# A mixture-of-experts trunk: the first expert's rows by one-hot products, and weights that no longer wait for a gather

## The reference, cut to what matters

```python
scores = softmax(xt @ router_w)                       # 512 x 16
sel = scores + router_bias
# best of 4 groups by the sum of its two best, then the two best experts in it
gates = two chosen scores, divided by their sum, 0 elsewhere
h = silu(xt @ w_gate[e]) * (xt @ w_up[e])             # 16 experts, 1024 -> 512
h = h * gates[:, e]
y = sum over e of h @ w_down[e]                       # 512 -> 1024
```

## Time and profile before

| | |
|---|---|
| median of three runs | 1234.52 us (1226.4 to 1235.66) |
| the profiled execution's own time | 1230.52 us |
| its span | 1228.8 us |
| PE busy | 1193.8 us (97%) |
| DVE, ACT, POOL busy | 893.2 us (73%), 703.7 us (57%), 183.9 us (15%) |
| DMA | 281.52 MB, 229 GB/s on average, 358 to 381 GB/s in most slices of the experts' loop |
| median from issue to landing of a half of up weights | 13.0 us |
| chain that ended last | PE 83%, DMA 7%, DVE 6% |

### The profile page before, as it was taken

How to read it: one execution, slowest core, us unless ns; L and a number is a source line. 1 busy time by engine, 2 the same in 40 slices (tenths; PEclk the granted TensorE clock), 3 DMA queues, 4 the chain that set the end, 5 groups by cost and what they waited for, 6 DMA issues and landing times.

```text
span 1228.8 us, 14990 instructions
## 1 busy us (share of the span) xinstructions
PE 1193.8 (97%) x5802; PEld 945.0 (77%) x5803; DVE 893.2 (73%) x1159; ACT 703.7 (57%) x866; POOL 183.9 (15%) x158
## 2 busy tenths in 40 slices
PE   7999999999999999999999999999999999999995
PEld 5787588877888888876887766768878888888873
DVE  5275555678999998989433555675679999998886
ACT  4432523357687786774333554573267778777672
POOL 1000100211132221210000000000212222122111
PEclk9999999999999999999899999999999999999998
DMA  8223021179999999987111420322289999999973
GB/s 286 71 85 122 1 103 70 52 257 411 358 368 378 368 370 377 358 340 281 69 70 52 154 86 18 103 84 88 78 314 381 373 362 376 379 367 371 370 276 137
DMA packets 66346, 281.52 MB, mean 229 GB/s; under 512 B 12854, under 2 KB 13110, under 8 KB 41698
## 3 DMA queue, kind: packets, MB, share of 16 engines
q1 hardware_dynamic: 49248, 247.55, 53.2%
q0 software_dynamic: 12288, 28.42, 8.1%
q10 hardware_dynamic: 4738, 4.57, 1.1%
HBM read 270.99 MB, written 25.20 MB: 241 GB/s over the span
## 4 chain that ended last, share of the span: by engine, by line
PE 83%; DMA 7%; DVE 6%; issue 2%; ACT 1%; POOL 0%; DVEq 0%; SPq 0%; ACTq 0%; POOLq 0%
PE ps L717 22%; PE ps L719 22%; PE ps L718 22%; DMA ring<-in_moe_w_up_dram 4%; PE ps L885 2%; PE ps L1168 2%; PE ps L1178 2%; DVE ring_r L1613 2%; PE ps L1191 2%; DMA ring<-in_moe_w_down_dram 1%; PE ps L894 1%; DMA ring<-in_kv_w_dram 1%; PE ps L822 1%; PE ps L1099 1%; PE ps L1087 1%
## 5 line engine op out<-in xcount | busy, mean ns | idle before, releaser
L1613 DVE TENSOR_TENSOR ring_r<-ring,ring_r 128x2048 fp32r<-128x2048 f32 x128 | 291.7, 2284 | 7.8 <-ACT ring_r L1346 7.8
L1346 ACT CAST ring_r<-ring 128x2048 fp32r<-128x2048 f32 x128 | 242.6, 1927 | 15.7 <-DMA ring<-in_moe_w_gate_dram 9.8
L718 PE MATMUL ps<-ring_r,xgT_r 128*128 128x512 f32 x528 | 205.9, 390 | 0.0
L1346 ACT CAST high_r<-ring 128x2048 fp32r<-128x2048 f32 x64 | 122.2, 1913 | 113.4 <-DMA ring<-in_moe_w_up_dram 113.4
L1613 DVE TENSOR_TENSOR ring_r<-ring,high_r 128x2048 fp32r<-128x2048 f32 x64 | 146.1, 2289 | 36.3 <-ACT high_r L1346 35.9
L613 POOL DMA_INDIRECT sum_rows<-arena,tokv x28 | 57.7, 2062 | 389.6 <-ACT arena L1399 389.6
L718 PEld LDWEIGHTS ps<-ring_r,xgT_r 128*128 128x128 f32 x528 | 99.3, 188 | 18.8
L717 PE MATMUL ps<-ring_r,xgT_r 128*128 128x512 f32 x272 | 109.1, 401 | 0.2 <-DVE ring_r L1613 0.2
L719 PE MATMUL ps<-ring_r,xgT_r 128*128 128x512 f32 x272 | 106.1, 390 | 0.0
L717 PE MATMUL ps<-high_r,xgT_r 128*128 128x512 f32 x256 | 102.9, 402 | 1.2 <-DVE xgT_r L1827 1.1
L717 PE MATMUL ps<-featT,ring_r 128*128 128x512 f32 x256 | 103.8, 405 | 0.0
(11 more groups left out here) (288 smaller groups left out, 2118.8 us busy)
## 6 DMA issues: line engine op xcount, KB each, us to landing
ring<-in_moe_w_gate_dram SPq DMA_DIRECT2D x64, 1024.0 KB, 12.2
ring<-in_moe_w_up_dram SPq DMA_DIRECT2D x64, 1024.0 KB, 13.0
ring<-in_moe_w_down_dram SPq DMA_DIRECT2D x64, 1024.0 KB, 12.4
ring<-in_gla_w_in_dram SPq DMA_DIRECT2D x6, 2048.0 KB, 9.8
ring<-in_kv_w_dram SPq DMA_DIRECT2D x4, 2048.0 KB, 12.8
ring<-in_fox_w_qg_dram SPq DMA_DIRECT2D x4, 2048.0 KB, 8.1
ring<-in_gla_w_out_dram SPq DMA_DIRECT2D x2, 2048.0 KB, 7.8
h_rows<-arena POOLq DMA_DIRECT2D x8, 512.0 KB, 2.9
```

What stands on the lines that cost most here:

```text
L718: pe.matmul(o, left[0], right[1], start=False, stop=False)
L1346: act.copy(high, w).then_inc(half_high, 1)
L1613: dve.tensor_tensor(low, w, high.bitcast(F32), ALU.subtract).then_inc(half_low, 1)
```

## The change

Four things are done together, in both layers.

1. `select`, the first part of the router, runs on tiles 0 and 1 (`EARLY = 2`) right after DVE has scaled tile 2, and on tiles 2 and 3 at the old place. Ranks and the one-hot of expert 0 are made in two parts too. In layer 1 PE does the logits of tiles 0 and 1 together after output unit 5. The router's scratch moves from the arena into the buffer `turned`.
2. Expert 0's rows are no longer gathered. PE multiplies `Hp` by the one-hot of expert 0 (`direct_rows`), which gives the rows already transposed: 16 products for tiles 0 and 1 in place of 20 idle products (3 stay), 16 for tiles 2 and 3 once their one-hot is there.
3. POOL gathers expert 1's rows after the direct products have read `Hp` and after its list is taken; expert 2's follow. Lists come from one table each, of four columns. The clearing of `xg` goes. Expert 0's and 2's tables are made by PE after the gate product of expert 0.
4. SP no longer waits for a gather before half 6. On ACT, halves 2 and 3 move ahead into the router.

```diff
@@ router scratch
+        EARLY = 2
+        ENTRY = (1, 2, 0)
@@ SP, experts
                         if n == 4:
                             sp.wait_ge(last_rows_stored, 32 * (L + 1))
-                        if n == 6:
-                            sp.wait_ge(gathered[0], 16 * (8 * L + 1))
@@ POOL, experts
-                pool.wait_ge(pads_clear, 2 * (L + 1))
+                pool.wait_ge(first_rows_stored, 32 * (L + 1))
+                pool.wait_ge(h_scaled, T * L + 2)
                 pool.wait_ge(last_rows_stored, 32 * (L + 1))
-                for e in range(3):
-                    pool.wait_ge(tbl_ev, 2 * E * L + e + 1)
-                    if e == 2:
-                        pool.wait_ge(xt_done, 2 * (E * L + 1))
+                pool.wait_ge(xt_done, 2 * (E * L + 1))
+                for n, e in enumerate(ENTRY[:2]):
+                    pool.wait_ge(tbl_ev, 2 * (E * L + n) + 1)
                     gather(xg[:, e % 2, :], tokv[:, e, 0:1], gathered[e % 2])
@@ PE
+            def direct_rows(kk, tiles):
+                for j in range(4):
+                    c = slice(j * P, (j + 1) * P)
+                    for t in tiles:
+                        mm = pe.matmul(ps[:, kk, c], Hp[:, t, (4 * kk + j) * P:(4 * kk + j + 1) * P],
+                                       onehot_of(0)[:, t * P:(t + 1) * P].bitcast(F32),
+                                       start=j == 0 and t == 0, stop=t == T - 1, skip_group_check=True)
+                return mm
@@ PE, entry_end
+                pe.wait_ge(rt_picked, 2 * L + 1)
+                pe.wait_ge(*taken(OUT_UNITS[L] + 6))
+                for t in range(EARLY):
+                    mm = rank(L, t)
+                mm.then_inc(rt_ranks, 1)
@@ PE, router
-                idle_products(20, 4)
-                pe.wait_ge(rt_picked, L + 1)
+                pe.wait_ge(early_hot, L + 1)
+                for kk in range(2):
+                    direct_rows(kk, range(EARLY))
+                idle_products(3, 4)
+                pe.wait_ge(rt_picked, 2 * L + 2)
...
-                idle_products(5, 4)
+                idle_products(4, 4)
@@ PE, experts
+                pe.wait_ge(hot, E * L + 1)
+                for kk in range(2):
+                    direct_rows(kk, range(EARLY, T)).then_inc(xt_done, 1)
                 pe.wait_ge(rt_info, 2 * (L + 1))
-                for e in range(3):
-                    pe.wait_ge(hot, E * L + e + 1)
-                    entry_table(e, slice(0, 2), ps[:, IDS_BANKS[e], 0:2]).then_inc(ids_done, 1)
-                    idle_products(2, 4)
                 pe.wait_ge(rt_ready, L + 1)
-                for e in range(3):
-                    entry_table(e, slice(2, 4), ps[:, 6, 2 * e:2 * e + 2]).then_inc(tbl_done, 1)
-                idle_products(5, 4)
-                pe.wait_ge(gathered[0], 16 * (8 * L + 1))
-                turn_rows(xg[:, 0, :], xt_done)
-                idle_products(4, 4)
+                entry_table(ENTRY[0])
...
                         wide(ps[:, 2, :], xgT[:, e % 2, :, :], "gate", e)
+                    if e == 0:
+                        entry_table(ENTRY[1])
+                        pe.wait_ge(rt_total, L + 1)
+                        entry_table(ENTRY[2])
@@ ACT, take_normed
+                    if t == 2:
+                        act.wait_ge(rt_in, 2 * L + 1)
+                        act.activation(rt[1][:, 0:EARLY, :], rt[0][:, 0:EARLY, :], ACT.Exp).then_inc(rt_exp, 1)
@@ ACT, router
+                high_half(L, 2)
+                act.wait_ge(rt_in, 2 * (L + 1))
...
+                high_half(L, 3)
@@ DVE, rows_normed
+                        if t == 2:
+                            select(L, 0, EARLY, 2 * L + 1)
+                take_ranks(L, 0, EARLY, 2 * L + 1)
+                one_hots4(dve, onehot_of(0)[:, 0:EARLY * P], early_hot, ranks[:, 0:EARLY, :], slot1, 0)
                 dve.wait_ge(rows_centred, T * L + T)
                 scale(N, T - 1)
@@ DVE, experts
-                take_ids(L, 2)
-                dve.wait_ge(tbl_done, E * L + 3)
-                for e in range(3):
-                    dve.tensor_reduce(tokg[:, e:e + 1], ps[:, 6, 2 * e:2 * e + 2], AX.X, ALU.add).then_inc(tbl_ev, 1)
+                take_rows(0)
+                take_entry(0)
                 low_half(L, 2)
-                take_rows(0)
                 low_half(L, 3)
+                take_entry(1)
+                take_entry(2)
                 low_half(L, 4)
                 low_half(L, 5)
```

More of the change, by code:

```diff
@@ L249, in yoco_trunk @@
         dummy = at(18000, P)
-        ranks = at(17792, T, E)
+        ranks = at(18464, T, E)
         spare = hT_hi[:, :, :].rearrange("p k s -> p (k s)")
@@ L261, in yoco_trunk, with router_part @@
         info = spare[:, 3 * BANK:3 * BANK + T * E * 4].rearrange("p (t e c) -> p t e c", t=T, c=4)
[L263 to L266, removed]
+        def router_part(n, width):
+            return turned[:, 5 + n // 4, n % 4 * T * E:n % 4 * T * E + width]
+        rt = [router_part(n, T * E).rearrange("p (t e) -> p t e", t=T) for n in range(12)]
+        rv = [at(18432 + 4 * n, T) for n in range(8)]
+        total = at(18528, E)[0:1, :]
         w_loaded = [sem(f"w_loaded{n}") for n in range(PAIRED)]
@@ L793, in tail, with rank @@
                 entry_end(L)
+            def rank(L, t):
+                bank = early_bank(L) if t < EARLY else 6
+                for s in range(t + 1):
+                    before = upto_b if s == t else ones_b
+                    mm = pe.matmul(ps[:, bank, t * E:(t + 1) * E], before[:, :], picked_b[:, s, :],
+                                   start=s == 0, stop=s == t)
+                return mm
[6 more added lines that the diff above has]
+                                       start=j == 0 and t == 0, stop=t == T - 1, skip_group_check=True)
+                return mm
             def idle_products(n, bank):
@@ L823, in logits @@
                                    rw[:, k, :], start=k == 0, stop=k == K - 1)
-                if t == T - 1:
+                if t in (EARLY - 1, T - 1):
                     mm.then_inc(rt_logits, 1)
             def router(L):
-                idle_products(20, 4)
-                pe.wait_ge(rt_picked, L + 1)
[L830 to L834, removed]
+                pe.wait_ge(early_hot, L + 1)
[3 more added lines that the diff above has]
+                pe.wait_ge(rt_picked, 2 * L + 2)
+                for t in range(EARLY, T):
+                    rank(L, t)
                 for s in range(T):
@@ new lines, in some @@
+                def some(v):
+                    return v[:, t0:t1, :]
+                peak, whole, best, chosen = (v[:, t0:t1] for v in (rv[0], rv[1], rv[3], rv[4]))
+                logits = some(rt[11])
+                dve.wait_ge(rt_logits, turn)
+                dve.wait_ge(ln_rstd, 2 * L * T + t1)
+                do(dve.tensor_tensor(logits, ps[:, 6, t0 * E:t1 * E].rearrange("p (t e) -> p t e", t=T_),
+                                     over_e(ln_r[:, t0:t1, 1]), ALU.mult))
+                do(dve.tensor_tensor(logits, logits, each_t(shift_logits[:, L, :], E), ALU.add))
@@ new lines, in select @@
+                do(dve.tensor_reduce(peak, logits, AX.X, ALU.max))
+                dve.tensor_tensor(some(rt[0]), logits, over_e(peak), ALU.subtract).then_inc(rt_in, 1)
+                dve.wait_ge(rt_exp, turn)
+                weights, sel = some(rt[1]), some(rt[3])
+                do(dve.tensor_reduce(whole, weights, AX.X, ALU.add))
+                do(dve.tensor_tensor(some(rt[2]), over_e(whole), each_t(rbias[:, :], E), ALU.mult))
+                do(dve.tensor_tensor(sel, weights, some(rt[2]), ALU.add))
@@ new lines, in take_ranks, with router, over_e @@
+            def take_ranks(L, t0, t1, turn):
+                dve.wait_ge(rt_ranks, turn)
+                bank = early_bank(L) if t1 <= EARLY else 6
+                do(dve.tensor_tensor(ranks[:, t0:t1, :],
+                                     ps[:, bank, t0 * E:t1 * E].rearrange("p (t e) -> p t e", t=t1 - t0),
+                                     rt[8][:, t0:t1, :], ALU.mult))
+            def router(L):
+                def over_e(v):
+                    return v.unsqueeze(2).to_broadcast([P, T, E])
+                turn = 2 * (L + 1)
+                select(L, EARLY, T, turn)
+                do(dve.tensor_tensor(rt[9], rt[1], rt[8], ALU.mult))
@@ L1779, in router @@
-                one_hots4(dve, onehot_of(2), hot, ranks, slot1, 2)
-                take_ids(L, 1)
                 do(dve.reciprocal(rv[6], rv[5]))
@@ L1785, in router @@
                                   ).then_inc(rt_ready, 1)
+                one_hots4(dve, onehot_of(2), hot, ranks, slot1, 2)
             def count_parts(L):
@@ L1816, in experts, with take_table, take_entry @@
                         dve.sem_inc(s, n)
-                def take_table(rows, gate, done):
-                    dve.tensor_scalar(rows, ps[:, 7, 0:2], BIG, None, ALU.add).then_inc(done, 1)
```

(8 more changed lines are left out.)

96 lines of the change are left out of this document (38 added, 58 removed).

## The result

The changed kernel takes 1242.91 us (median of 4 runs, 1239.74 to 1246.03), the kernel before 1231.51 (4 runs, 1226.4 to 1235.66). The ratio is 1.0088, with a 95% interval of 1.0063 to 1.0113: slower by 0.9%, where I had forecast slightly faster. (The ratio is the recorded one; the two medians alone give 1.0093.) The time is inside my range of 1220 to 1243, though only by 0.1 us, and the direction is not what I forecast. The profiled execution took 1239.74 us with a span of 1238.0, against 1230.52 and 1228.8: +9.2.

A forecast was written before the change was run, and what follows sets the result against it. PE (busy 97%) and DMA were taken to bound the kernel nearly alike. Layer terms -1.0 and -1.9, together -2.9 us, gave 1227.6 from the profiled execution, 1231.6 from the median; forecast 1230 between them, range 1220 to 1243.

The forecast's parts named there:

- The early selection and tile 3: Router on DVE: selecting early delays tile 3's second half by 0.9 us in layer 0, nothing in layer 1.
- The direct products and gate 0: Entry: early 16 products take 3.55 us, late selection starts at 255.4, gate 0 at 265.6 instead of 269.83.
- rival C: Entry: short products replacing wide idle ones lower the clock, about +4 to +11 us, 1236 to 1242; chance 0.07.
- The landing: Expert 1's gather lands 9.0 us after issue; rows 0.3 us later in layer 0, 1.0 earlier in layer 1.
- rival B: Between gate 0 and up 0: weights and residual ahead of the gather, landing 13.4 us, 1239 to 1243; chance 0.16.
- My own mark for it: Sign at PE's wait for expert 1's gather: over 5 us means released weights and residual delay it.
- Rival A: Expert 1's gather slips past queued weights as queues take turns, landing in 6 us; about 1222 us, chance 0.22.
- The clock behind the wait: After PE's wait for expert 1's gather, half-speed work might cost 1.5 us; 0.7 per layer taken.
- The loops: Second half of the expert loops: late waits for hidden rows go, -2.0 us in layer 0, -1.6 in layer 1.
- The lead on the queue: DMA, with half 6 unheld and expert 0's gather saved, runs 3 to 5 us ahead, removing late waits.

The follow-up runs named there:

- e2: Changed kernel, but ACT issues the residual stores only once expert 1's gather has landed; weights run free. 1234.39 us, ratio 1.001.
- e5: Changed kernel with layer 1's logits of tiles 0 and 1 taken one unit apart again; 1241.58 us, ratio 1.0082.
- e10: Changed kernel with weight halves from half 6 on held only until GpSimd begins issuing expert 1's gather; 1243.92 us, ratio 1.0102.
- e3: Changed kernel with both halves from 6 on and residual stores held until expert 1's gather has landed; 1237.67 us, ratio 1.0059.
- e6: Changed kernel with 26 unused 128x512 products where PE waits for expert 1's gather, in both layers; 1238.88 us, ratio 1.0065.
- e1: Changed kernel, but SP again holds half 6 and all behind it until expert 1's gather has landed; 1232.95 us, ratio 1.0011.
- e11: Changed kernel with halves from half 6 on held until PE has done the last of three entry tables; 1233.1 us, ratio 1.0003.
- e9: Kernel before, with the second mixer's 64 narrow forget-gate products spread, 16 behind each of four units; 1228.09 us, ratio 0.9977.

## Why the prediction was wrong

**The early selection and tile 3: right.** The last half of tile 3 is taken at 248.47; I had written 249.0, so 0.4 us late instead of 0.9.

**The direct products and gate 0: nearly right.** The late ones, 32 records, take 3.63 us, where the earlier trace rows had given 3.55. Gate 0 starts at 267.11, not 265.6: the clock was low from 251.7 to 255.1, the 16 logits products of the last tile took 2.35 us, and the late selection began at 256.46, not 255.4. I had listed that clock risk as rival C and put nothing in the sum. It belongs to the change in layer 0: of the eight profiles in which PE idles 0.9 us ahead of tile 3's transposes, seven show a low stretch there, and of the six others, with an idle of 0.2 us or with 8 products ahead of them, none. In layer 1 e2, e5 and e10 show one of 10.2 us at 897, whose cause is open. Measured from the last add of tile 3, layer 1 is as forecast: 17.1 us to gate 0 against 16.7.

**The landing: this is the step that failed.** "I take 9.0 us": measured 11.0 and 12.8. Transposes in layer 0 were forecast 0.3 us later than before; they came 3.8 later: 1.4 from the later issue, 2.0 from the landing. In layer 1, measured from tile 3, they were forecast 1.0 earlier and came 3.0 later: 0.2 and 3.8. So of the 12.1 us between my sum (-2.9) and the profile (+9.2), 5.8 are the landing. I had the right row before me: the gather for expert 2, about 11 us behind the same weights and stores. I then took off 1.8 us for 0.7 MB less ahead of it, and in layer 1 took 9.0 again. That deduction assumed a line that moves up as bytes go. The queues of the changed kernel in 272 to 274 and 276 to 278 show something else:

```profile
q10 hardware_dynamic: 226, 0.84, 104.2%
q0 software_dynamic: 1, 0.00, 0.5%
q1 hardware_dynamic: 1, 0.00, 0.0%
```

```profile
q1 hardware_dynamic: 81, 0.61, 76.2%
q0 software_dynamic: 61, 0.11, 16.2%
q10 hardware_dynamic: 15, 0.06, 7.0%
```

The gather was issued at 268.13, and its first packet moves 5.8 us later, at 273.98. On empty queues that start took 2.9 us (e3), so the company costs 2.9 us there; from 274 on the gather shares with weights and stores, at a sixth to a quarter of the time. So it pays twice, for what was posted before it and for what runs beside it. Layer 1 shows that "before" doesn't mean before the issue: ACT issued its four stores at 911.73 to 913.52, behind the gather's 911.46, and they still went first. The queues there in 916 to 918, where q0 has no row:

```profile
q10 hardware_dynamic: 220, 0.79, 97.3%
q1 hardware_dynamic: 10, 0.06, 6.9%
```

The gather's own instruction on GpSimd takes 2.26 us, where it took 0.99. That is not the load on the queues. Its row in the changed kernel, the row of DVE beside it, and its row in e3, where no packet of any queue moved in that time:

```profile
268.13 2.26 POOL L606 DMA_INDIRECT arena<-h_rows,tokv  x1 [12.57 <-DVE tokg L1866]
267.11 4.48 DVE L1641 TENSOR_TENSOR ring_r<-ring,ring_r 128x2048 fp32r<-128x2048 f32 x2
266.63 2.26 POOL L608 DMA_INDIRECT arena<-h_rows,tokv  x1 [10.94 <-DVE tokg L1869]
```

In the entries it goes with DVE's long subtractions for the low halves: with one running all through it the instruction takes 2.3 to 2.8 us, otherwise 1.0 to 1.1 (as at 264.11 in the kernel before). The first packet moved some 0.6 us after its end in e2, in e3 and in the kernel before, so about 1.1 us of the landing may come from this; no run moved the subtraction, so it is not shown.

This was rival B, with its place and its mechanism as written. My own mark for it, a wait over 5 us, was met too (5.5 and 7.3). I had set its threshold at 9.5 us of landing, half a microsecond above my own estimate, and given it 0.16 against 0.55: two numbers that don't go together. Its time of 1239 to 1243 doesn't follow from its +7.5 to +11 either, which from the median give up to 1245.5. That the range held the measured 1242.91 is luck.

Rival A's rule (the Trainium skill, DMA: Bandwidth & Descriptors, Queues, rings and completion order), that each engine goes round the rows that have work, is half borne out. From 274 to 278 three queues do take turns, and by that a gather needs no empty queue. In 272 to 274 they do not, though weights (half 8, issued at 270.16) and gather had both been issued; whether the engines had them as work by then, no view shows.

**The clock behind the wait: the full price.** I took 0.7 of 1.5 us per layer. The sum took half of the bound, and that half was mis-sized. From the transposes to the hidden rows of expert 0 it is 8.17 and 8.19 us where it was 6.59 and 6.60: 1.6 each, the bound of 1.5 and not its half. e6, with its wait filled, has 6.66 in layer 1.

**The loops: right in layer 0, half right in layer 1.** -2.4 of -2.0 and -0.7 of -1.6 us. The lead on the queue that I counted as a gain was the same thing as the gather's delay: e1 takes it away and the loops take 1.4 and 1.6 us more, while the entries take 4.2 and 7.4 us less.

**The second mixer: not costed at all.** The sum has no term for it. The change joins two short runs of narrow products into one of 3.6 us, and in the profiled execution the low stretch behind it cost 1.5 us; the other 1.6 of the +3.1 are the longer stretch near 610, which is not shown to be the change's.

## What to carry to other kernels

When the first consumer of a gather is made earlier, the next gather becomes the critical one: look at what is on all queues at the moment of its issue, take its landing from the row that had the same company, and don't discount it. A hold on bulk transfers can be cheap: ended 5.6 us after the gather's issue it was (e11); ended 0.8 us ahead of the issue it does nothing (e10), and on both queues until the landing the loop pays it back (e3). Keep TensorE at wide products while it waits, but not for longer than the wait (e6, layer 0), and don't put narrow products together in long runs: cut up among wide ones, the same 64 cost 0.2% of this kernel less.

## What the hardware showed that I had not expected

A gather has a start that no empty queue removes: 2.9 us from issue to first packet in e2 and e3, of which 2.26 are GpSimd's instruction. In e2 it was issued at 271.57, and in 272 to 274 the whole core moved

```profile
DMA packets 0, 0.00 MB, mean 0 GB/s; under 512 B 0, under 2 KB 0, under 8 KB 0
```

while its first packets are in 274 to 276. The shortest landing of the entry's first gather is 4.5 us in the kernel before and in e9, and 5.4 in e3.

A granted clock of 0.50 costs 0.45 us per us where PE is full with wide and narrow work mixed, a little under half. The low stretches in these profiles last 3.4, 6.8 or 10.2 us, and the length does not follow from the edit: the same idle of 0.9 us ahead of tile 3's transposes went with 3.4 us in the changed kernel and in e1, with 10.2 us in e2, e5 and e6, and with none in e3. That is a spread of some 4 us (10.2 at 0.45) between profiles of nearly the same program. Executions of one program show it too: e2's twelve went from 1226.48 us, with a mean granted clock of 0.991, to 1240.11 us with 0.979. So a single profile should not settle an edit worth 4 us.
